# First attention of a 256-token transformer: pairs of heads one by one, or in units of two pairs

## The chip, the cores and the metric

The kernel runs on one core of one Trainium2 chip. The metric is the device time of one execution in microseconds. Three runs of the kernel before took 984.9, 985.58 and 985.37 us, median 985.37.

## The reference, cut to what matters

Three blocks follow one another on a sequence of 256 tokens of width 1024: attention with an MLP, a recurrent block with an MLP, and a block with three mixers. The change touches only the first attention, with 16 heads of 64:

```python
qkv = jnp.einsum('bsd,de->bse', h, w_qkv).reshape(B, S, 3, N_HEADS, HEAD_DIM)
...
s = jnp.einsum('bqhd,bkhd->bhqk', q_c, k_band).astype(jnp.float32) * scale + bias
s = jnp.where(key_pos[None, None, None, :] >= 0, s, NEG_INF)
p = jax.nn.softmax(s, axis=-1).astype(v_band.dtype)
return jnp.einsum('bhqk,bkhd->bqhd', p, v_band)
...
return jnp.einsum('bsd,de->bse', o, w_o)
```

Its output is added to `h`. The normalised `mem_2`, needed much later, is split beside the attention.

## The kernel before

Weights arrive as tiles of 1 MB through five buffers. ScalarE rounds each half of a tile to `hi` (L837) and VectorE makes the rest `lo` (L1357); a product is hi times hi, hi times lo and lo times hi. A tile of `wk` or `wq` gives two blocks of 128 features, one a "half" (`half`, L340 and L348: eight matmuls of 512 columns, eight of 256); its result leaves the bank as a copy on ScalarE (`bt`, L868) and a sum on VectorE (`joined`, L1371 and L1373), then a scaling on GpSimd (L2004). A tile of `wo` is applied in two halves of twelve matmuls of 512 columns (L295 to L297) that add into banks 0 to 3.

Five instruction streams are written by hand, one for each engine, and each engine runs its own strictly in its order; they meet at semaphores. A PSUM bank is claimed by `fill`, which makes TensorE wait until the reader of the bank's last content has released it.

The attention runs in nine steps over `ATTN_TILES` (three pairs of `wk`, `wq` tiles, then three `wo` tiles), two halves a step. Step j does, on TensorE (loop at L540): a half; the values of pair j - 2 (`pair_av`, L531, bank 7, 256 columns); the scores of pair j (`pair_scores`, L520, one head in bank 4, the other in bank 6); the three transposes of head 2j - 2 (`turn`, L470, bank 5); the other half; the transposes of head 2j - 1. A head's scores cover the causal part: 256 queries' worth in 384 columns. They pass through VectorE (bias and row minimum, L1490), ScalarE (exponential with sum, L922), VectorE (reciprocal and scaling, L1427 and L1430), TensorE (transposes), ScalarE (copy to `PT`, L927), TensorE (values), ScalarE (`oh`, L978) and VectorE (`ol`, L1476). Two buffers `L` and two `PT` hold one head each.

In every half the ScalarE stream (loop at L970) is: split a chunk of the coming weights, `bt` of this half, `oh`, the copy of transposes, the exponentials of one head, in steps 4 to 7 one square of `mem` (L879), which GpSimd adds up (L1999). The VectorE stream (loop at L1478) is: the `lo` chunk, bias and minimum of one head, `joined`, `ol`, in every second half `split_low` of `mem` (L1377), softmax of that head. After the ninth step come the values of pair 7, the sum of the squares of `mem` and the last `wo` tile.

Of the kernel before, what the change touches and what calls it, by code (L numbers as in the profile page):

```python
# [8 lines left out]
P = 128  # L9
S = 256  # L10
# [56 lines left out]
CROSS = [(256, 0), (0, 128), (384, 256), (128, 384)]  # L67
ROWS_ADDED = {"wo": 0, "w2_0": 4, "rout": 8, "w2_1": 12}
ATTN_TILES = [(name, i) for i in range(1, 4) for name in ("wk", "wq")] + [("wo", i) for i in range(3)]
DSA_STEPS = [[("dq", 3, 0), ("dq", 3, 1)], [("xq", 0, 0), ("xq", 0, 1)]]  # L70
DSA_STEPS += [[("xq", i, j)] for i in range(1, 4) for j in range(2)] + [[("gz", 0, 0)], [("gz", 0, 1)]]
INDEX_STEPS = [("dk", 0), ("dk", 1), ("dq", 0), ("dq", 1)]
# [18 lines left out]
def build(nc, A, out):  # L91
    ctx = ExitStack()

    def sem(name):
        return ctx.enter_context(nc.semaphore(name))
# [17 lines left out]
    h_added, ssq_made, ms_made, tok_rstd, hn_made = sem("h_added"), sem("ssq_made"), sem("ms_made"), sem("tok_rstd"), sem("hn_made")  # L113
    u_scaled, h_normed, bt_made = sem("u_scaled"), sem("h_normed"), sem("bt_made")
    sp_log, sp_made = sem("sp_log"), sem("sp_made")
    exp_made, p_made, o_high = sem("exp_made"), sem("p_made"), sem("o_high")
    z_made, z_high, z_low = sem("z_made"), sem("z_high"), sem("z_low")
    tap_made, xc_made, t_made = sem("tap_made"), sem("xc_made"), sem("t_made")
    gi_made, a_made, aa_made, mass_made, root_made, drive_made = (
# [23 lines left out]
    def place(name, off, free, dt=F32):  # L143
        return nc.alloc_sbuf_tensor_at(name, [P] + list(free), dt, offset=off)
# [8 lines left out]
    def slot(name, i, free=(NC, S), dt=F32, off=0):  # L153
        return place(name, o_slot[i] + off, free, dt)
# [46 lines left out]
    T = slot("T", 8, [16, 256])  # L201
    gw = slot("gw", 14, [2, NC, P])
    both = [place(f"both{i}", o_tmp + 2048 + 1536 * i, [384]) for i in range(2)]
    mk, mv = slot("mk", 3), slot("mv", 4, [2, D])
    bo = slot("bo", 6, [D], off=4096)
    zf = [slot(f"zf{i}", 5, [S], off=1024 * i) for i in range(4)]
# [66 lines left out]
    def pe():  # L273
# [192 lines left out]
        def turn(n, blocks, b=5):  # L466
            p.wait_ge(p_made, n + 1)
            done = fill(("turn", n), b)
            for src, dst in blocks:
                m = PE.transpose(bank[b][:, dst:dst + P], L[n % 2][:, src:src + P], ident[:, :])  # L470
            m.then_inc(done, 1)

        def weigh(n, o, V, a, b):
# [34 lines left out]
        cols("wq", 0, X2, (7, 6))  # L508
        for b in range(4):
            p.wait_ge(*free["wv", b])  # L510
        def pair_scores(j):

            p.wait_ge(kq_scaled, 4 * (j // 2) + 2 + j % 2)
            if j == 0:
                p.wait_ge(q_scaled, 1)
            done = [fill(("s", 2 * j + e), (4, 6)[e]) for e in range(2)]
            for a, b, n, c in ((P, S, S, 0), (0, P, P, 256)):
                for e in range(2):
                    r = slice(64 * e, 64 * e + 64)
                    m = PE.matmul(bank[(4, 6)[e]][:, c:c + n], q[r, j, a:b], k[r, j, 0:n], start=True, stop=True, skip_group_check=True)  # L520
                    if c:
                        m.then_inc(done[e], 1)

        def pair_av(j):
            for e in range(2):
                p.wait_ge(*free["turn", 2 * j + e])
            done = fill(("av", j), 7)
            for kb, c, e_ in ((0, 0, 256), (1, 256, 384)):
                for e in range(2):
                    n = 2 * j + e  # L530
                    m = PE.matmul(bank[7][64 * e:64 * e + 64, S - (e_ - c):S], v[:, kb, n * 64:n * 64 + 64], PT[e][:, c:e_],  # L531
                                  start=kb == 0, stop=kb == 1, skip_group_check=True)
            m.then_inc(done, 1)

        def wo(i, cs=(0, 1)):
            for k_ in range(2):
                p.wait_ge(freed[7], free["av", 2 * i + k_][1])
                rows("wo", i, 4, oh[:, 2 * i:2 * i + 2, :], ol[:, 2 * i:2 * i + 2, :], cs, (k_,), 0 if len(cs) == 1 else 1)

        for j in range(9):  # L540
            name, i = ATTN_TILES[j]
            if name == "wo":
                wo(i, (1,))
            else:
                half(name, i, 0, X2, 0)
            if j >= 2:
                pair_av(j - 2)
            if j < 8:
                pair_scores(j)
            if j:  # L550
                turn(2 * j - 2, CAUSAL)
            if j == 8:
                turn(15, CAUSAL, 4)
            if name == "wo":
                wo(i, (0,))
            else:
                half(name, i, 1, X2, 1)
            if 0 < j < 8:
                turn(2 * j - 1, CAUSAL)
        pair_av(7)  # L560
        total("mem", 7)
        wo(3)

# [253 lines left out]
    def act():  # L817
# [25 lines left out]
        def at_half(name, i, j):  # L843
            hi_to(2 * (T_OF[name, i] + HIS - 1) + j + 1)
# [80 lines left out]
        def turned(n, width):  # L925
            a.wait_ge(*full["turn", n])
            ACTE.activation(PT[n % 2][:, 0:width], bank_of["turn", n][:, 0:width], ACT.Copy).then_inc(free["turn", n][0], 1)  # L927
# [34 lines left out]
        for j in range(2):  # L962
            second("wq", j, scale=0.125)

        def turned_pair(n):
            if n >= 2:
                a.wait_ge(*full["av", n // 2 - 1])
            turned(n, 384)

        for j in range(9):  # L970
            name, t = ATTN_TILES[j]
            for e in range(2):
                at_half(name, t, e)
                if name != "wo":
                    second(name, 2 * t + e, scale=0.125 if name == "wq" else 1.0)
                if e == 0 and j >= 2:
                    a.wait_ge(*full["av", j - 2])
                    ACTE.activation(oh[:, j - 2, :], bank[7][:, 0:S], ACT.Copy).then_inc(o_high, 1)  # L978
                if e == 0 and j:
                    turned_pair(2 * j - 2)  # L980
                if e and j:
                    turned_pair(2 * j - 1)
                if j < 8:
                    n = 2 * j + e
                    a.wait_ge(*free["s", n])
                    soft(n, TT)
                if 4 <= j < 8:
                    square("mem", [mem[:, n, :] for n in range(NC)], 2 * (j - 4) + e)
        a.wait_ge(*full["av", 7])
        ACTE.activation(oh[:, 7, :], bank[7][:, 0:S], ACT.Copy).then_inc(o_high, 1)  # L990
        at_tile("wo", 3)
        inverse_root("mem")

# [184 lines left out]
        for i in range(10):  # L1178
            for name, t, j in DSA_STEPS[i]:
                at_half(name, t, j)  # L1180
                if name != "gz":
                    second(name, 2 * t + j, scale={"dq": 128 ** -0.5, "xq": 1.0 / 16}[name])
            if 1 <= i <= 8:
                n = i - 1
                a.wait_ge(*full[("av", 7) if n < 2 else ("dav", n - 2)])
                turned(16 + n, 384)
            if i < 8:
                a.wait_ge(*free["s", 16 + i])
                soft(16 + i, TT)
            n = i - 2  # L1190
            if n >= 0:
                a.wait_ge(*free["dav", n])
                ACTE.activation(yh[:, n, :], tmp[n % 2][:, :], ACT.Copy).then_inc(d_high, 1)
# [146 lines left out]
    def dve():  # L1340
# [23 lines left out]
        def at_half(name, i, j):  # L1364
            lo_to(2 * (T_OF[name, i] + 1) + j + 1)
# [105 lines left out]
        DVE.tensor_tensor(q[:, 0, :], q[:, 0, :], rstd["mix0"][:, :], ALU.mult).then_inc(q_scaled, 1)  # L1471
        joined(q[:, 1, :], "wq", 1, scale=0.125)

        def o_low(j):
            d.wait_ge(o_high, j + 1)
            DVE.tensor_tensor(ol[:, j, :], bank[7][:, 0:S], oh[:, j, :].bitcast(F32), ALU.subtract).then_inc(freed[7], 1)  # L1476

        for j in range(9):  # L1478
            name, t = ATTN_TILES[j]
            for e in range(2):  # L1480
                at_half(name, t, e)
                if j < 8:
                    i = 2 * j + e
                    Lb, s_ = L[e], stat[:, i % 16, :]
                    d.wait_ge(*full["s", i])
                    d.wait_ge(toep_cut, i // 4 + 1)
                    if j:
                        d.wait_ge(*full["turn", i - 2])
                    for m, (c, f, b0) in enumerate([(0, 256, 0), (256, 384, 128)]):
                        x = DVE.tensor_tensor_reduce(out=Lb[:, c:f], in0=bank_of["s", i][:, c:f], in1=T[:, i, b0:256], scale=-1.0,  # L1490
                                                     scalar=3.4e38, op0=ALU.add, op1=ALU.min, accum_out=s_[:, m:m + 1])
                    x.then_inc(free["s", i][0], 1)
                if name == "wk":
                    joined(k[:, 2 * t + e, :], "wk", 2 * t + e)
                if name == "wq":
                    joined(q[:, 2 * t + e, :], "wq", 2 * t + e, scale=0.125)
                if e == 0 and j >= 2:
                    o_low(j - 2)
                if e == 1 and j < 8:
                    split_low("mem", mem[:, j, :], mh, ml, "g_mem_2", j)  # L1500
                if j < 8:
                    soft(i, TT)
        o_low(7)
        lo_to(2 * (T_OF["wo", 3] + 2))
        by_token("mem", 2)

# [674 lines left out]
```

## Time and profile before

| | |
|---|---|
| median of 3 runs | 985.37 us |
| span of the profiled execution | 984.4 us |
| TensorE matmul busy in it | 977.1 us, 99% |
| VectorE, ScalarE, GpSimd busy | 682.6, 585.1, 66.2 us |
| mean granted TensorE clock | 0.998 |
| the attention's steps on TensorE | 42.6 to 111 us |

An engine's busy time is the sum of its instructions. The rows that follow further down come from five views: the page's chain (which work, followed back from the last instruction, made up the span), the same chain in order of time, stretches with the busy time of each engine, timelines of one engine, and groups of instructions by line. A matmul's row lasts longer than its step, since matmuls are pipelined, so in timelines the distance between starts is the cost.

### The profile page before, as it was taken

Reading aid. Unit: us, or ns where it says so; the run is one execution under the profiler, and the core shown is the slowest. Engines: PE = TensorE matmul, PEld = TensorE weight load, DVE = VectorE, ACT = ScalarE, POOL = GpSimd, SP = SyncE. Lnnn points to the kernel's source line nnn. Section 1 sums busy time; section 2 is a strip of 40 time slices with the busy share of each in tenths; the row PEclk is TensorE's granted clock in tenths of the full one; section 3 lists DMA queues with packets and bytes.
Section 4 is the critical chain, followed back from the end, with each engine's and each line's share of the span. In section 5 each row is a group of like instructions: output and inputs, shape, how many; then the busy total and the mean of one; then the engine's idle time right before and its main releaser. Section 6 shows DMA issues by size and latency. Waiting matters only on the chain.

```text
span 984.4 us, 13450 instructions
## 1 busy us (share of the span) xinstructions
PE 977.1 (99%) x5186; PEld 828.7 (84%) x5186; DVE 682.6 (69%) x1159; ACT 585.1 (59%) x1026; POOL 66.2 (7%) x80
## 2 busy tenths in 40 slices
PE   9999999999999999999999999999999999999997
PEld 6887888888888998888888888888888777988886
DVE  5887776655667889766556678778577355787564
ACT  6777755444547896654445476557766354685443
POOL 1323110000000241000000000000020000000000
PEclk9999999999999999999999999999999999999999
DMA  9753555554555445555645556445533543336551
GB/s 364 308 195 129 171 174 211 198 205 175 200 185 173 170 161 181 177 208 174 227 177 200 185 196 248 171 171 190 195 129 137 186 148 128 129 129 208 179 190 43
DMA packets 27119, 180.33 MB, mean 183 GB/s; under 512 B 2992, under 2 KB 3888, under 8 KB 6320
## 3 DMA queue, kind: packets, MB, share of 16 engines
q1 hardware_dynamic: 26336, 176.98, 50.3%
q0 software_dynamic: 288, 2.10, 0.6%
q8 instruction: 41, 0.67, 0.3%
q10 hardware_dynamic: 432, 0.39, 0.1%
q14 instruction: 22, 0.18, 0.0%
HBM read 178.41 MB, written 1.05 MB: 182 GB/s over the span
## 4 chain that ended last, share of the span: by engine, by line
PE 99%; DMA 1%; DVE 0%; ACT 0%; SPq 0%; issue 0%; DVEq 0%
PE bank L340 25%; PE bank L295 16%; PE bank L297 16%; PE bank L296 16%; PE bank L348 13%; PE bank L310 1%; PE bank L470 1%; PE bank L486 1%; PE bank L591 1%; PE bank L520 1%; PE bank L311 1%; PE bank L531 1%; DMA front<-in_front 1%; PE bank L462 1%; PE bank L706 0%; PE bank L722 0%
## 5 line engine op out<-in xcount | busy, mean ns | idle before, releaser
L1357 DVE TENSOR_TENSOR lo<-raw,hi 128x1024 fp32r<-128x1024 f32 x318 | 375.9, 1228 | 20.0 <-ACT hi L837 20.0
L837 ACT ACTIVATE hi<-raw 128x1024 fp32r<-128x1024 f32 x318 | 320.2, 1050 | 96.9 <-PE bank L297 95.1
L340 PE MATMUL bank<-X,hi 128*128 128x512 f32 x1016 | 267.0, 395 | 0.0
L340 PEld LDWEIGHTS bank<-X,hi 128*128 128x128 f32 x1016 | 185.0, 189 | 33.2 <-issue 0.4
L348 PEld LDWEIGHTS bank<-X,lo 128*128 128x128 f32 x1016 | 138.5, 190 | 10.1
L348 PE MATMUL bank<-X,lo 128*128 128x256 f32 x1016 | 141.6, 282 | 0.0
L868 ACT ACTIVATE bt<-bank 128x256 f32<-128x256 f32 x135 | 51.0, 380 | 142.7 <-PE bank L340 134.3
L1371 DVE TENSOR_TENSOR zr<-bank,bt 128x256 f32<-128x256 f32 x64 | 27.1, 424 | 109.0 <-ACT bt L868 109.0
L295 PE MATMUL bank<-hi,zh 128*128 128x512 f32 x256 | 100.0, 391 | 0.0
L297 PE MATMUL bank<-hi,zl 128*128 128x512 f32 x256 | 99.8, 390 | 0.0
L296 PE MATMUL bank<-lo,zh 128*128 128x512 f32 x256 | 99.6, 389 | 0.0
L295 PE MATMUL bank<-hi,X 128*128 128x512 f32 (+1 forms) x176 | 67.9, 386 | 0.0
L297 PE MATMUL bank<-hi,X 128*128 128x512 f32 (+1 forms) x176 | 66.9, 380 | 0.0
L296 PE MATMUL bank<-lo,X 128*128 128x512 f32 (+1 forms) x176 | 66.9, 380 | 0.0
L297 PEld LDWEIGHTS bank<-hi,zl 128*128 128x128 f32 x256 | 48.1, 188 | 10.4
L296 PEld LDWEIGHTS bank<-lo,zh 128*128 128x128 f32 x256 | 48.1, 188 | 10.2
L295 PEld LDWEIGHTS bank<-hi,zh 128*128 128x128 f32 x256 | 48.2, 188 | 8.9
L1012 ACT ACTIVATE zh<-zf 128x256 fp32r<-128x256 f32 x64 | 26.6, 415 | 21.2 <-DVE zf L1528 21.2
L297 PEld LDWEIGHTS bank<-hi,X 128*128 128x128 f32 x176 | 33.1, 188 | 6.4
L295 PEld LDWEIGHTS bank<-hi,X 128*128 128x128 f32 x176 | 33.1, 188 | 6.2 <-issue 0.3
L296 PEld LDWEIGHTS bank<-lo,X 128*128 128x128 f32 x176 | 33.1, 188 | 5.9
L922 ACT ACTIVATE L<-L,stat 128x256 f32<-128x256 f32 (+1 forms) x56 | 25.5, 456 | 20.4 <-DVE stat L1490 9.8
(344 smaller groups left out, 1428.3 us busy)
## 6 DMA issues: line engine op xcount, KB each, us to landing
raw<-in_w SPq DMA_DIRECT2D x64, 1024.0 KB, 4.7
raw<-in_rin SPq DMA_DIRECT2D x8, 1024.0 KB, 4.7
raw<-in_wk SPq DMA_DIRECT2D x4, 1024.0 KB, 11.0
raw<-in_wq SPq DMA_DIRECT2D x4, 1024.0 KB, 9.4
raw<-in_wo SPq DMA_DIRECT2D x4, 1024.0 KB, 4.7
raw<-in_mk SPq DMA_DIRECT2D x4, 1024.0 KB, 4.8
raw<-in_mv SPq DMA_DIRECT2D x4, 1024.0 KB, 4.7
raw<-in_rout SPq DMA_DIRECT2D x4, 1024.0 KB, 4.8
```

The lines of the kernel that those rows point to most:

```text
L295: PE.matmul(o, ah, bh, start=start, stop=False)
L296: PE.matmul(o, ah, bl, start=False, stop=False)
L297: return PE.matmul(o, al, bh, start=False, stop=stop)
L310: PE.matmul(bank[b][:, :], wh[:, c:c + P], both_, start=k_ == 0, stop=False, skip_group_check=True)
L340: return PE.matmul(bank[b][:, :], wh[:, c:c + P], x[:, k_, :, :].rearrange("p a b -> p (a b)"), start=k_ == 0, stop=k_ == NC - 1, skip_gro ...
L348: PE.matmul(bank[b][:, 0:S], wl[:, c:c + P], x[:, k_, 0, :], start=False, stop=False, skip_group_check=True)
L837: ACTE.activation(hi[u_ % HIS][:, c], raw[u_ % RAW][:, c], ACT.Copy).then_inc(hi_cut, 1)
L868: ACTE.activation(bt[n % BT][:, :], bank_of[key][:, S:2 * S], func, scale=scale, **kw).then_inc(bt_made, 1)
L922: i = ACTE.activation(Lb[:, c:e], Lb[:, c:e], ACT.Exp, scale=-1.0, bias=s_[:, m:m + 1], accum_out=s_[:, 2 + m:3 + m])
L1012: ACTE.activation(zh[i % 3][:, j, :], zf[c % 4][:, :], ACT.Copy).then_inc(z_high, 1)
L1357: DVE.tensor_tensor(lo[u_ % RAW][:, c], raw[u_ % RAW][:, c], hi[u_ % HIS][:, c].bitcast(F32), ALU.subtract).then_inc(lo_cut, 1)
L1371: DVE.tensor_tensor(dst, first, rest, ALU.add).then_inc(free[key][0], 1)
```

## The change

The 18 halves are numbered x. Heads now go in units: pairs (0, 1), (2, 3), (4, 5), (6), (7). A unit's scores are issued together, the first pair's in banks 4 and 6, the second's in banks 2 and 3, at x = 1, 5, 9, 13 and, for the last, 14. The values of a unit are issued together at x = 5, 9, 13, 16 and 17, 512 columns of bank 7 for two pairs; ScalarE's `oh` and VectorE's `ol` take them in one instruction each, with a semaphore `o_low` for `wo` and bank 7. There are four buffers for probabilities and four for their transposes (`L4`, `PT4`), the new ones where `hx` was. Transposes stand at the ends of halves or, for the last head of a unit, in the middle of one; the tables say where. VectorE and ScalarE take heads by the table `HEADS_AT`. The mixer that follows waits for unit 4 instead of pair 7. The core of the diff:

```diff
+ATTN_UNITS = [(0, 1), (2, 3), (4, 5), (6,), (7,)]
+UNIT_OF = {j: u for u, pairs in enumerate(ATTN_UNITS) for j in pairs}
+SCORES_AT = {1: (0, 1), 5: (2, 3), 9: (4, 5), 13: (6,), 14: (7,)}
+HEADS_AT = {1: (0,), 2: (1, 2), 3: (3,), 5: (4,), 6: (5, 6), 7: (7,), 9: (8,), 10: (9, 10), 11: (11,), 13: (12,), 14: (13,), 15: (14, 15)}
+TURN_IN = {5: 3, 9: 7, 13: 11, 16: 13, 17: 15}
+TURN_AT = {3: ((0, 5),), 4: ((1, 5), (2, 4)), 7: ((4, 5),), 8: ((5, 5), (6, 4)), 11: ((8, 5),), 12: ((9, 5), (10, 4)),
+           15: ((12, 5),), 16: ((14, 4),)}
+UNIT_AT = {5: 0, 9: 1, 13: 2, 16: 3, 17: 4}
...
+    L4 = L + [slot(f"L{i}", 3, [512], off=2048 * (i - 2)) for i in (2, 3)]
+    PT4 = PT + [slot(f"PT{i}", 3, [512], off=2048 * i) for i in (2, 3)]
...
+            src_ = L4[n % 4] if n < 16 else L[n % 2]
             for src, dst in blocks:
-                m = PE.transpose(bank[b][:, dst:dst + P], L[n % 2][:, src:src + P], ident[:, :])
+                m = PE.transpose(bank[b][:, dst:dst + P], src_[:, src:src + P], ident[:, :])
...
-        def pair_scores(j):
+        def pair_scores(j, banks):
...
-            done = [fill(("s", 2 * j + e), (4, 6)[e]) for e in range(2)]
+            done = [fill(("s", 2 * j + e), banks[e]) for e in range(2)]
...
-        def pair_av(j):
-            for e in range(2):
-                p.wait_ge(*free["turn", 2 * j + e])
-            done = fill(("av", j), 7)
-            for kb, c, e_ in ((0, 0, 256), (1, 256, 384)):
-                for e in range(2):
-                    n = 2 * j + e
-                    m = PE.matmul(bank[7][64 * e:64 * e + 64, S - (e_ - c):S], v[:, kb, n * 64:n * 64 + 64], PT[e][:, c:e_],
-                                  start=kb == 0, stop=kb == 1, skip_group_check=True)
+        def unit_av(u):
+            pairs = ATTN_UNITS[u]
+            for n in range(2 * pairs[0], 2 * pairs[-1] + 2):
+                p.wait_ge(*free["turn", n])
+            done = fill(("av", u), 7, (o_low, u + 1))
+            for o, j in enumerate(pairs):
+                for kb, c, e_ in ((0, 0, 256), (1, 256, 384)):
+                    for e in range(2):
+                        n = 2 * j + e
+                        m = PE.matmul(bank[7][64 * e:64 * e + 64, o * S + S - (e_ - c):o * S + S], v[:, kb, n * 64:n * 64 + 64],
+                                      PT4[n % 4][:, c:e_], start=kb == 0, stop=kb == 1, skip_group_check=True)
             m.then_inc(done, 1)
...
+            for k_ in ks:
+                p.wait_ge(o_low, UNIT_OF[2 * i + k_] + 1)
...
-        for j in range(9):
-            name, i = ATTN_TILES[j]
-            if name == "wo":
-                wo(i, (1,))
-            else:
-                half(name, i, 0, X2, 0)
-            if j >= 2:
-                pair_av(j - 2)
-            if j < 8:
-                pair_scores(j)
-            if j:
-                turn(2 * j - 2, CAUSAL)
-            if j == 8:
-                turn(15, CAUSAL, 4)
-            if name == "wo":
-                wo(i, (0,))
-            else:
-                half(name, i, 1, X2, 1)
-            if 0 < j < 8:
-                turn(2 * j - 1, CAUSAL)
-        pair_av(7)
+        for x in range(18):
+            name, i = ATTN_TILES[x // 2]
+            e = x % 2
+            for part in range(2):
+                if part and x in TURN_IN:
+                    turn(TURN_IN[x], CAUSAL)
+                if name == "wo":
+                    wo(i, (1 - e,), (part,))
+                elif x in TURN_IN:
+                    half(name, i, e, X2, e, range(4 * part, 4 * part + 4))
+                elif part:
+                    half(name, i, e, X2, e)
+            for n, b in TURN_AT.get(x, ()):
+                turn(n, CAUSAL, b)
+            if x in UNIT_AT:
+                unit_av(UNIT_AT[x])
+            for o, j in enumerate(SCORES_AT.get(x, ())):
+                pair_scores(j, ((4, 6), (2, 3))[o])
...
+        def turned_head(n):
+            if n >= 4:
+                a.wait_ge(*full["av", UNIT_OF[n // 2 - 2]])
+            a.wait_ge(*full["turn", n])
+            ACTE.activation(PT4[n % 4][:, 0:384], bank_of["turn", n][:, 0:384], ACT.Copy).then_inc(free["turn", n][0], 1)
+
+        def head_soft(n):
+            Lb, s_ = L4[n % 4], stat[:, n, :]
+            a.wait_ge(*free["s", n])
+            for m, (c, e) in enumerate(TT):
+                i = ACTE.activation(Lb[:, c:e], Lb[:, c:e], ACT.Exp, scale=-1.0, bias=s_[:, m:m + 1], accum_out=s_[:, 2 + m:3 + m])
+            i.then_inc(exp_made, 1)
+
+        for x in range(18):
+            name, t = ATTN_TILES[x // 2]
+            e = x % 2
+            at_half(name, t, e)
+            if name != "wo":
+                second(name, 2 * t + e, scale=0.125 if name == "wq" else 1.0)
+            if x in TURN_IN:
+                turned_head(TURN_IN[x])
+            for n, _ in TURN_AT.get(x, ()):
+                turned_head(n)
+            if x in UNIT_AT:
+                pairs = ATTN_UNITS[UNIT_AT[x]]
+                a.wait_ge(*full["av", UNIT_AT[x]])
+                ACTE.activation(oh[:, pairs[0]:pairs[-1] + 1, :].rearrange("p a b -> p (a b)"), bank[7][:, 0:S * len(pairs)],
+                                ACT.Copy).then_inc(o_high, 1)
+            for n in HEADS_AT.get(x, ()):
+                head_soft(n)
+            if 8 <= x < 16:
+                square("mem", [mem[:, n, :] for n in range(NC)], x - 8)
...
+        def unit_low(u):
+            pairs = ATTN_UNITS[u]
+            r = slice(pairs[0], pairs[-1] + 1)
+            d.wait_ge(o_high, u + 1)
+            DVE.tensor_tensor(ol[:, r, :].rearrange("p a b -> p (a b)"), bank[7][:, 0:S * len(pairs)],
+                              oh[:, r, :].rearrange("p a b -> p (a b)").bitcast(F32), ALU.subtract).then_inc(o_low, 1)
+
+        def head_soft(n):
+            Lb, s_ = L4[n % 4], stat[:, n, :]
+            d.wait_ge(exp_made, n + 1)
+            step(DVE.reciprocal(s_[:, 4:6], s_[:, 2:4]))
+            own()
+            for m, (c, e) in enumerate(TT):
+                i = DVE.tensor_scalar(Lb[:, c:e], Lb[:, c:e], s_[:, 4 + m:5 + m], None, ALU.mult)
+            i.then_inc(p_made, 1)
+
+        for x in range(18):
+            name, t = ATTN_TILES[x // 2]
+            e = x % 2
+            at_half(name, t, e)
+            for i in HEADS_AT.get(x, ()):
+                Lb, s_ = L4[i % 4], stat[:, i, :]
+                d.wait_ge(*full["s", i])
+                d.wait_ge(toep_cut, i // 4 + 1)
+                if i >= 4:
+                    d.wait_ge(*full["turn", i - 4])
+                for m, (c, f, b0) in enumerate([(0, 256, 0), (256, 384, 128)]):
+                    y = DVE.tensor_tensor_reduce(out=Lb[:, c:f], in0=bank_of["s", i][:, c:f], in1=T[:, i, b0:256], scale=-1.0,
+                                                 scalar=3.4e38, op0=ALU.add, op1=ALU.min, accum_out=s_[:, m:m + 1])
+                y.then_inc(free["s", i][0], 1)
+            if name == "wk":
+                joined(k[:, 2 * t + e, :], "wk", 2 * t + e)
+            if name == "wq":
+                joined(q[:, 2 * t + e, :], "wq", 2 * t + e, scale=0.125)
+            if x in UNIT_AT:
+                unit_low(UNIT_AT[x])
+            if e == 1 and x < 16:
+                split_low("mem", mem[:, x // 2, :], mh, ml, "g_mem_2", x // 2)
+            for i in HEADS_AT.get(x, ()):
+                head_soft(i)
```

## Rows read from the trace of the kernel before

**Rows 1.** The page: chain that ended last, shares by engine.

```profile
PE 99%; DMA 1%; DVE 0%; ACT 0%; SPq 0%; issue 0%; DVEq 0%
```

**Rows 2.** Stretches: us; busy of PE, PEld, DVE, ACT, POOL; clock, DMA, GB/s.

```profile
42.60:111.00 68.40, 68.40 (x428) 54.74 (x428) 53.12 (x157) 48.49 (x126) 17.53 (x24) 1.00 0.47 165
```

**Rows 3.** The chain in order of time, in the stage: start, us, what.

```profile
43.54 1.82 PE bank L340 x7
...
56.62 0.80 PE bank L531 x8
57.42 0.85 PE bank L520 x8
58.28 0.48 PE bank L470 x3
58.76 1.62 PE bank L340 x7
...
61.56 0.33 PE bank L470 x3
```

**Rows 4.** Timeline of PE, a value group, then scores: start, us, what.

```profile
56.55 0.44 PE L531 MATMUL bank<-PT,v 128*64 128x256 f32 x2
56.82 0.39 PE L531 MATMUL bank<-PT,v 128*64 128x256 f32 x2
57.03 0.39 PE L531 MATMUL bank<-PT,v 128*64 128x128 f32 x4
57.35 0.49 PE L520 MATMUL bank<-k,q 64*128 64x256 f32 x2
```

**Rows 5.** The chain again: two groups of transposes behind values.

```profile
105.96 0.86 PE bank L470 x6
```

**Rows 6.** Timeline of PEld: the weight loads of that value group.

```profile
56.55 0.63 PEld L531 LDWEIGHTS bank<-PT,v 128*64 128x64 f32 x8 [0.26 <-issue]
```

**Rows 7.** Timeline of ACT: exponential, weight chunk, bt, copy of transposes.

```profile
51.50 0.51 ACT L922 ACTIVATE L<-L,stat 128x256 f32<-128x256 f32 x1 [0.30 <-DVE stat L1490]
...
52.39 1.04 ACT L837 ACTIVATE hi<-raw 128x1024 fp32r<-128x1024 f32 x1
53.51 0.38 ACT L868 ACTIVATE bt<-bank 128x256 f32<-128x256 f32 x1
53.84 0.49 ACT L927 ACTIVATE PT<-bank 128x384 f32<-128x384 f32 x1
```

**Rows 8.** Timeline of DVE: softmax, weight chunk, reduction, join, split.

```profile
52.52 0.17 DVE L1427 RECIPROCAL stat<-stat 128x2 f32<-128x2 f32 x1 [0.72 <-ACT L L922]
...
53.19 1.22 DVE L1357 TENSOR_TENSOR lo<-raw,hi 128x1024 fp32r<-128x1024 f32 x1
54.32 0.42 DVE L1490 CUSTOM_DVE_ANT_0 L<-bank,T 128x256 f32<-128x256 f32 x1
...
54.87 0.42 DVE L1373 SCALAR_TENSOR_TENSOR q<-bank,bt 128x256 f32<-128x256 f32 x1
55.21 0.48 DVE L1377 SCALAR_TENSOR_TENSOR M<-mem,vec,M 128x256 fp32r<-128x256 f32 x1
```

**Rows 9.** 512 columns: timeline of ACT; groups of DVE by line.

```profile
116.97 0.63 ACT L896 ACTIVATE junk<-h 128x512 f32<-128x512 f32 x1 [2.15 <-DVE h L1403]
...
L1403 DVE TENSOR_TENSOR h<-bank,h 128x512 f32<-128x512 f32 x4 | 2.5, 680 | 0.0
```

**Rows 10.** Timelines of POOL and DVE: a sum beside the softmax.

```profile
93.30 0.80 POOL L1999 TENSOR_TENSOR sq<-sq,sq 128x256 f32<-128x256 f32 x1 [1.36 <-ACT sq L879]
...
93.15 1.03 DVE L1430 TENSOR_SCALAR L<-L,stat 128x256 f32<-128x256 f32 x2
```

**Rows 11.** Stretches behind the last matmul; timeline of PE at the start.

```profile
978.00:981.00 3.00, 1.33 (x6) 0.75 (x5) 0.93 (x4) 1.18 (x4) 0.00 (x0) 1.00 0.16 59
981.00:984.40 3.40, 0.00 (x0) 0.00 (x0) 1.30 (x2) 0.00 (x0) 0.00 (x0) 0.55 0.41 154
...
1.33 3.78 PE L498 MATMUL bank<-warm 128*128 128x512 f32 x4 [1.33 <-POOL warm L2006]
```

More of the change, by code:

```diff
@@ L115, in build @@
     sp_log, sp_made = sem("sp_log"), sem("sp_made")
-    exp_made, p_made, o_high = sem("exp_made"), sem("p_made"), sem("o_high")
+    exp_made, p_made, o_high, o_low = sem("exp_made"), sem("p_made"), sem("o_high"), sem("o_low")
     z_made, z_high, z_low = sem("z_made"), sem("z_high"), sem("z_low")
@@ L519, in pair_scores @@
                     r = slice(64 * e, 64 * e + 64)
-                    m = PE.matmul(bank[(4, 6)[e]][:, c:c + n], q[r, j, a:b], k[r, j, 0:n], start=True, stop=True, skip_group_check=True)
+                    m = PE.matmul(bank[banks[e]][:, c:c + n], q[r, j, a:b], k[r, j, 0:n], start=True, stop=True, skip_group_check=True)
                     if c:
                         m.then_inc(done[e], 1)
-        def pair_av(j):
-            for e in range(2):
-                p.wait_ge(*free["turn", 2 * j + e])
-            done = fill(("av", j), 7)
-            for kb, c, e_ in ((0, 0, 256), (1, 256, 384)):
-                for e in range(2):
-                    n = 2 * j + e
-                    m = PE.matmul(bank[7][64 * e:64 * e + 64, S - (e_ - c):S], v[:, kb, n * 64:n * 64 + 64], PT[e][:, c:e_],
-                                  start=kb == 0, stop=kb == 1, skip_group_check=True)
+        def unit_av(u):
[9 more added lines that the diff above has]
+                                      PT4[n % 4][:, c:e_], start=kb == 0, stop=kb == 1, skip_group_check=True)
@@ L533, in pair_av, with wo @@
             m.then_inc(done, 1)
-        def wo(i, cs=(0, 1)):
-            for k_ in range(2):
-                p.wait_ge(freed[7], free["av", 2 * i + k_][1])
+        def wo(i, cs=(0, 1), ks=(0, 1)):
+            for k_ in ks:
+                p.wait_ge(o_low, UNIT_OF[2 * i + k_] + 1)
                 rows("wo", i, 4, oh[:, 2 * i:2 * i + 2, :], ol[:, 2 * i:2 * i + 2, :], cs, (k_,), 0 if len(cs) == 1 else 1)
-        for j in range(9):
-            name, i = ATTN_TILES[j]
-            if name == "wo":
-                wo(i, (1,))
-            else:
-                half(name, i, 0, X2, 0)
-            if j >= 2:
-                pair_av(j - 2)
-            if j < 8:
-                pair_scores(j)
-            if j:
-                turn(2 * j - 2, CAUSAL)
-            if j == 8:
-                turn(15, CAUSAL, 4)
-            if name == "wo":
-                wo(i, (0,))
-            else:
-                half(name, i, 1, X2, 1)
-            if 0 < j < 8:
-                turn(2 * j - 1, CAUSAL)
@@ L963, in act @@
             second("wq", j, scale=0.125)
[L965 to L988, printed above, removed]
@@ L989, in act @@
-        a.wait_ge(*full["av", 7])
-        ACTE.activation(oh[:, 7, :], bank[7][:, 0:S], ACT.Copy).then_inc(o_high, 1)
+        def turned_head(n):
[9 more added lines that the diff above has]
+            i.then_inc(exp_made, 1)
@@ L1184, in act @@
                 n = i - 1
-                a.wait_ge(*full[("av", 7) if n < 2 else ("dav", n - 2)])
+                a.wait_ge(*full[("av", 4) if n < 2 else ("dav", n - 2)])
                 turned(16 + n, 384)
@@ L1472, in dve @@
         joined(q[:, 1, :], "wq", 1, scale=0.125)
[L1474 to L1502, printed above, removed]
@@ L1503, in dve @@
-        o_low(7)
+        def unit_low(u):
[12 more added lines that the diff above has]
+            i.then_inc(p_made, 1)
```

## The prediction

> **What bounds the kernel now.** I read the chain that ended last first: TensorE holds 99% of it [rows 1]. Then the table of stretches: from 42.6 to 111 us, the stage that the change rewrites, TensorE is busy in all of the 68.40 us at granted clock 1.00, with VectorE at 53 us and ScalarE at 48 [rows 2]. The view of waits names no matmul of this stage that waits for another engine. So the stage lasts as long as the sum of TensorE's steps, and every wait that is put into TensorE's stream is added to the run, because nothing behind it has slack. The question is what the change takes off these steps and where it makes TensorE wait for an engine that was hidden until now.
>
> The chain in order of time shows the rhythm of one pair [rows 3]: values (AV) 0.80, scores (S) 0.85, transposes (T) 0.48, a half of a weight tile 2.80 (58.76 to 61.56), T again, 0.33, another half. A pair takes 8.09 us.
>
> **What regrouping takes off TensorE.** The count of matmuls stays. What changes is how often TensorE goes from full tiles to half tiles and back. Inside a value group the starts lie 0.27, then 0.21 apart, and the two short passes with the exit take 0.32 [rows 4]. A pass over 256 columns in its stride is thus 0.21 and one over 128 half of that, 0.11: a pair run on behind another of its kind should take 0.64. An AV group then carries 0.80 - 0.64 = 0.16 of switching, an S group 0.85 - 0.64 = 0.21, and T behind S 0.48 - 0.33 = 0.15. Where S is followed by a half instead, the half's first seven matmuls take 1.82 instead of 1.62, so 0.20. Before there are 8 AV and 8 S groups, 7 of the S followed by T and 1 by a half. After it there are 5 of each (units of two, two, two, one, one), all S followed by halves.
> AV saves 3 x 0.16 = 0.48, S 3 x 0.21 = 0.63, and the exits 7 x 0.15 + 0.20 - 5 x 0.20 = 0.25. Two more places have two T back to back, the second of which costs 0.38 instead of 0.33 (0.86 - 0.48) [rows 5]: minus 0.10. Sum: 1.26, call it 1.25 us. Bounds: 0.75 if run-on AV pairs keep their 0.16, 1.6 if exits cost no more than now.
>
> The Trainium skill speaks against a part of this: TensorE: Matmul & The Clock Gate (Part 3, The mechanism) says that a weight load overlaps a running matmul only where the row group differs. The value matmuls use all 128 rows, so by that rule their loads would lie bare and a second AV pair would still cost 0.80, which makes the saving 0.75. Against it stands the trace, where eight such loads are busy 0.63 us under one AV group whose passes still start 0.21 apart [rows 6]; I go by the trace.
>
> **What the new order makes TensorE wait for.** I number the halves x = 0 to 17. Two things move: the T of a unit's last head now stands in the middle of the half right ahead of the unit's AV, and four heads' scores come at once into four banks while VectorE and ScalarE take them one or two per half.
>
> (1) x = 5 and x = 9. TensorE: four k of the half, T(3) (or 7), four k, then the AV of both pairs, which needs the copy PT of that last head. ScalarE's own order at that x is: split the next weight chunk, then `bt` of this same half, and only then the copy of T. `bt` needs the half's last matmul. So the copy can't start before the half has ended, though T ended 1.4 us earlier. Results appear 0.17 after the next matmul could have started (a matmul's 0.40 against a step of 0.23), then `bt` 0.33 (53.51 to 53.84), the copy 0.49 [rows 7], and about 0.1 for the two signals: 1.1 us, of which 0.1 is the entry step that was counted. 1.0 us each, 2.0 together. Before, a whole half of 2.80 and more lay between this T and its AV. Behind the waiting AV stand the scores and the next half; ScalarE and VectorE have nothing else to do in the meantime. This one I hold for nearly sure: bounds 0.8 and 1.3 each.
>
> (2) x = 12. The scores of pair 5 lie in banks 2 and 3, and `wo` opens banks 2 and 3 at x = 12. Head 11 leaves bank 3 by VectorE's reduction, which stands in VectorE's block 11. Count from the end of the scores at x = 9. TensorE: two halves, T(8), and three matmuls into bank 2: 2.80 + 2.80 + 0.33 + 3 x 0.23 (seven matmuls of 512 columns take 1.62) [rows 3] = 6.6. VectorE, from -0.5 (the first pair's scores are done early): reduction 0.55, join 0.34, difference of 512 columns 0.68, split 0.48, softmax 0.67 [rows 8, 9], which makes 2.2. The square of `mem` runs on GpSimd beside it, and where it does the two multiplications of the softmax take 1.03 instead of 0.55 [rows 10]: 2.7. Then the weight chunk 1.13, heads 9 and 10 reduced 1.10, which ends at 4.9. ScalarE starts head 9's exponentials at 4.4 and takes 0.90 a head [rows 7], so head 10's end at 6.2; its softmax 0.67 to 1.15, the next chunk 1.13, head 11's reduction 0.55: 8.5 to 9.0. Wait 1.9 to 2.4. Before, each half had one head; now three heads' work stands between these scores and bank 3. I take 2.0 (bounds 0.5 and 2.5, since small overlaps make it shorter).
>
> (3) x = 14. Pair 7 takes the same banks 4 and 6 as pair 6 one half earlier. TensorE has 12 matmuls of `wo` between, 2.8, and the entry, 0.1. VectorE has: reduction 12 at 0.1, 0.55; the difference 0.68; split 0.48; softmax 0.67 to 1.15; weight chunk 1.13; reduction 13, 0.55: 4.2 to 4.6 [rows 8 to 10]. Wait 1.3 to 1.7; I take 1.5 (bounds 0.5 and 1.8).
>
> (4) x = 16. From the end of T(12) ScalarE does its copy 0.49, two heads' exponentials 1.8, a square (256 columns, as `bt`) 0.4, a weight chunk 1.0 and the copy of T(13) 0.49, with signals 4.3. TensorE does 6 matmuls, T(13), 6 matmuls, T(14): 1.4 + 0.33 + 1.4 + 0.33, and wants the values of pair 6 at 3.5. Wait 0.7 to 0.8, I take 0.7 (bounds 0 and 1.2). At x = 13 the same sum comes out without a wait, since the wait at x = 12 has let ScalarE catch up; x = 17 has only one copy ahead of it.
>
> What is late next: after each wait VectorE and ScalarE have caught up, as the four sums above include; the weight chunks stay a tile ahead on ScalarE and half a tile on VectorE, and the loads of weights wait for TensorE's use of tiles, which comes in the same order. The new semaphore `o_low` costs nothing: `wo` reads a unit only half a unit later. One copy and one difference of 512 columns instead of two of 256 [rows 9] saves these engines about 0.1 each per unit, which is off TensorE's path.
>
> **Sum.** 1.0 + 1.0 + 2.0 + 1.5 + 0.7 = 6.2 us of waits against 1.25 saved: +4.95. The profiled span is 984.4, so 989.35; the runs' median, 985.37, stands 1.0 above that span, so **990.3 us**, 0.5% slower.
>
> **Rivals.**
> A, the forecast, 988.3 to 991.8: all five waits come as counted, give or take the bounds. Chance 0.63.
> B: the banks come free in time and only the two copies behind `bt` wait: +2.0 - 1.25 = +0.75, 986.1. For it: VectorE is busy 53 of 68 us only, and every chain of (2) to (4) starts from an adding up of many steps. Against: these idle times lie where an engine waits for the other, and the chain of one softmax through both engines does not get shorter. 0.15.
> C, the other side: not slower. The deeper buffers hide all copies, as four instead of two buffers suggest, and only the switching is seen: 984.1. It decides at the point where ScalarE's copy of T(3) comes ahead of the half's end; the code's order speaks against it. With exits as cheap as now 983.8, and only something unseen in the steps could take it under 983.4. 0.10.
> D: the clock falls at the wait of x = 12. After the last matmul, which ended 1.33 us behind 978, the stretch from 981 shows a mean clock of 0.55: it fell in a pause of some two microseconds or more. At the start four passes of 512 columns take 3.78 us, about double of what 0.21 per 256 makes (1.7) [rows 11]. If it fell once and stayed down for some 4 us of work, as long as these four passes, that costs 1.9 more: 992.2. Against: the longest wait that I count is 2.0, at the near edge of that pause. 0.12.
>
> **Chances and range.** A difference of 0.2%, 983.4 to 987.3, is about what a measurement of this kernel can tell. Faster: 0.04 out of C. Same: 0.06 of C and 0.12 of B. Slower: A, D and the rest of B, 0.78. The range has to take in A, B and most of D: 985.9 to 992.6, with C and the far end of D left out.
>
> **What would show it.** In the profile of after, TensorE's rows at the first AV group should carry an idle time of about 1 us, released by ScalarE's PT copy, twice; `wo`'s fourth matmul an idle time released by VectorE's reduction; the scores of pair 7 the same; and AV runs of 16 passes should take 1.44 and S runs 1.49 in the chain. No idle at the AV would put me wrong on (1) and make it C; idle at the AV alone makes it B; a column PEclk under 1.00 in the stage makes it D. A saving other than 1.25 shows in the lengths of the groups themselves.

## The result, and the profile after

| | before | after |
|---|---|---|
| runs, median (lowest to highest) | 985.38 us (984.9 to 985.58, 4 runs) | 991.26 us (990.35 to 992.22, 4 runs) |
| ratio to before, 95% interval | | 1.0059 (1.0047 to 1.0072) |
| span of the profiled execution | 984.4 us | 989.0 us |
| the stage on TensorE (below) | 67.69 us | 72.44 us |

The change makes the kernel slower by 0.6%, where 0.5% was forecast (990.3 us).

The stage is measured in the chain, from the first scores to the sum of the squares of `mem`. Before it is

```profile
42.69 0.85 PE bank L520 x8
...
110.38 0.63 PE bank L458 x2
```

67.69 us from start to start. After it is

```profile
45.41 1.51 PE bank L531 x16
...
115.05 0.63 PE bank L468 x2
```

69.64, and the half of a tile that now stands ahead of the first scores, 2.80, belongs to it: 72.44, or 4.75 more. From there to the last matmul both kernels take 868.6 us. The whole loss lies in the stage.

The kernel before was not quite free of waits here. Its view of waits names no matmul, but two weight loads of L295 with 0.3 us each. One timeline row of such a load, and the two steps of the chain that are longer than the usual 0.23:

```profile
95.37 0.19 PEld L295 LDWEIGHTS bank<-hi,oh 128*128 128x128 f32 x1 [0.28 <-DVE lo L1357]
...
95.52 0.35 PE bank L295
103.65 0.36 PE bank L295
```

The timeline puts the first down to the `lo` chunk of VectorE and ties the second to no event; a `lo` chunk (102.18, 1.21 long) ends just ahead of that one too. Together they cost 0.25 us, which is needed below.

The view of waits of the kernel after has these (engine, line, what released it: us in total, times, longest):

```profile
PE bank L531 <- DVE stat L1517: 1.9, 1, 1.9
PE bank L544 <- issue: 1.8, 2, 0.9
PE bank L305 <- DVE stat L1517: 1.4, 1, 1.4
...
PE bank L544 <- ACT PT L979: 0.5, 1, 0.5
```

The scores of pair 7 wait for VectorE's reduction (x = 14), two value groups wait 0.9 each (x = 5 and 9), `wo`'s fourth matmul waits for a reduction (x = 12), the values of pair 6 for a copy (x = 16). The timelines of TensorE at x = 5 and x = 12 (start, us, what, idle before and releaser):

```profile
59.25 0.39 PE L350 MATMUL bank<-X,hi 128*128 128x512 f32 x1
60.54 1.52 PE L544 MATMUL bank<-PT,v 128*64 128x256 f32 x16 [0.90 <-issue]
...
86.85 0.40 PE L307 MATMUL bank<-hi,ol 128*128 128x512 f32 x1
88.67 0.51 PE L305 MATMUL bank<-hi,oh 128*128 128x512 f32 x1 [1.42 <-DVE stat L1517]
```

The cost of a wait is the distance of the starts less the ordinary step. At x = 5 that is 1.29 - 0.33 = 0.96; "issue" there means that the profile ties the wait to no event, but ScalarE's timeline shows what TensorE stood for:

```profile
59.68 0.38 ACT L878 ACTIVATE bt<-bank 128x256 f32<-128x256 f32 x1 [0.91 <-PE bank L350]
59.96 0.48 ACT L979 ACTIVATE PT<-bank 128x384 f32<-128x384 f32 x1
```

ScalarE is idle for 0.91 until the half ends, does `bt`, then the copy, which ends at 60.44; TensorE goes on at 60.54. At x = 12 the cost is 1.82 - 0.23 = 1.59, and the next step is 0.11 longer than usual in restarting.

What answers to [rows 3] in the chain after: the value and score groups of two pairs, and two groups of transposes in a row.

```profile
55.85 0.66 PE bank L481 x6
...
60.54 1.52 PE bank L544 x16
62.06 1.51 PE bank L531 x16
```

### The profile page after: what moved, and what is told of

Same layout as the page of the kernel before. It is cut to its first block, busy times and chain, and to the rows that moved or that the text cites. A ratio compares the mean times of both kernels' runs of the same rounds, so it can differ in the third digit from the quotient of the medians.

```text
span 989.0 us, 13441 instructions
## 1 busy us (share of the span) xinstructions
PE 976.4 (99%) x5186; PEld 829.2 (84%) x5186; DVE 683.1 (69%) x1156; ACT 583.7 (59%) x1023; POOL 69.3 (7%) x80
## 3 DMA queue, kind: packets, MB, share of 16 engines
HBM read 178.41 MB, written 1.05 MB: 181 GB/s over the span
## 4 chain that ended last, share of the span: by engine, by line
PE 97%; DVE 1%; ACT 1%; DMA 1%; issue 0%; SPq 0%; DVEq 0%
PE bank L350 25%; PE bank L305 16%; PE bank L307 16%; PE bank L306 16%; PE bank L358 13%; PE bank L320 1%; PE bank L481 1%; PE bank L497 1%; PE bank L601 1%; PE bank L321 1%; PE bank L544 1%; DMA front<-in_front 1%; PE bank L472 1%; PE bank L531 1%; PE bank L716 0%
## 5 line engine op out<-in xcount | busy, mean ns | idle before, releaser
L1561 DVE TENSOR_TENSOR zl<-zf,zh 128x256 fp32r<-128x256 f32 x64 | 26.9, 421 | 4.8 <-ACT zh L1028 3.3
```

What stands on the lines that cost most here:

```text
L1561: DVE.tensor_tensor(zl[i % 3][:, j, :], zf[c % 4][:, :], zh[i % 3][:, j, :].bitcast(F32), ALU.subtract).then_inc(z_low, 1)
```

## The experiments

Each starts from the kernel after the change unless it says otherwise. "Stage" is measured as above, 72.44 in the kernel after. All edits stand at the same places of the three loops.

**The copy ahead of `bt`.** ScalarE:

```diff
             at_half(name, t, e)
+            if x in (5, 9):
+                turned_head(TURN_IN[x])
             if name != "wo":
                 second(name, 2 * t + e, scale=0.125 if name == "wq" else 1.0)
-            if x in TURN_IN:
+            if x in TURN_IN and x > 9:
                 turned_head(TURN_IN[x])
```

> The kernel after the change, with one edit in ScalarE's order: at x = 5 and x = 9 the copy of the transposes of heads 3 and 7 comes ahead of `bt` of the same half. Theory (TensorE waits there only because the copy stands behind `bt`): both idle times of 0.90 us ahead of the value groups vanish, a value group starts 0.33 us behind the half's last matmul, and the span falls from 989.0 by 2 x 0.96 to about 987.1. Rival (the copy is late for another reason, or the time is lost again further on, at the banks of x = 12 and 14): the span stays near 989.0, with longer waits at `wo` and at the scores of pair 7.

Measured: the wait at x = 5 is gone (a step of 0.33), that at x = 9 is down to 0.10; the stage falls by 1.83 to 70.61, and the waits of 1.4, 1.9 and 0.5 stay as they are. The span is 988.1, since the opening of this execution was longer: its first scores start at 46.30, not 45.41, behind a wait of 2.0 for the first weights. The runs give 989.18 (988.29 to 992.65). The order on ScalarE is the cause of these two waits, and in the stage nothing of them comes back.

**The other banks.** TensorE:

```diff
-                pair_scores(j, ((4, 6), (2, 3))[o])
+                pair_scores(j, ((2, 3), (4, 6))[o] if x == 9 else ((4, 6), (2, 3))[o])
```

> The kernel after the change, with one edit in TensorE's stream: at x = 9 the scores of pair 4 go to banks 2 and 3 and those of pair 5 to banks 4 and 6, so that heads 8 and 9, which VectorE takes first, lie in the banks that `wo` opens at x = 12. Theory (the wait of 1.42 us idle ahead of `wo`'s fourth matmul is bank 3, held by head 11): it vanishes, 1.69 us. But that wait has also let ScalarE catch up: added up from the trace of after, the copy of T(9) then ends 0.2 after T(11) wants bank 5, and the copy of T(11) 0.45 after the values of unit 2 could start, so 0.65 comes back at x = 13 and the span is 988.0. Rival (waits are independent): nothing comes back and the span is 987.3. Rival (VectorE's lag, not the bank, is what counts): no gain, 989.0.

Measured: `wo`'s fourth matmul waits no more, but the seventh does, for the low part of its weight chunk. It starts 0.58 behind the sixth in place of 0.23:

```profile
87.56 0.50 PE L305 MATMUL bank<-hi,oh 128*128 128x512 f32 x1 [0.19 <-DVE lo L1373]
```

With 0.11 for the longer step behind it that costs 0.46, so the bank was worth 1.24 of 1.70. Something did come back, but at x = 12 and from VectorE; the two waits that I had added up for x = 13 did not appear. The expectation's size was nearly right (1.05) and its mechanism wrong. The stage of this execution is 72.74 all the same: behind the wait at x = 14 its clock fell, which is told below. The runs give 990.27.

**Head 13 together with head 12.**

```diff
-HEADS_AT = {... 13: (12,), 14: (13,), 15: (14, 15)}
+HEADS_AT = {... 13: (12, 13), 15: (14, 15)}
```

> The kernel after the change, with one edit in the table of heads: VectorE and ScalarE take head 13 together with head 12, at x = 13 instead of x = 14. Theory (the scores of pair 7 wait 1.9 us for bank 6, whose reduction stands behind softmax 12 and a weight chunk): that wait vanishes and the span is 987.1; the wait of 0.55 at x = 16 stays. Rival (the scores of pair 7 wait for something else, such as bank 4 or the scaling of q): 989.0.

Measured: no wait at the scores of pair 7, the others as before. The stage is 70.51, 1.93 less. The runs give 988.99 (988.38 to 989.31), 2.9 above the kernel before on the same chip, where the kernel after lay 5.9 above it at first and 5.05 when it was measured once more. The edit moves only the reduction that frees bank 6, so bank 6 was what they waited for.

**All three, and ScalarE's copies ahead of its weight chunk in the halves of `wo`** (x = 12, 13, 16 and 17; by the edit at x = 15 too).

> The kernel after the change with the three edits of the other runs together, and with ScalarE's copies of transposes ahead of its weight chunk at x = 12, 13, 16 and 17. The order of TensorE's work is that of after but for the banks. Theory (the change costs 6.1 us in waits and saves about 1.5 in switching between full and half tiles): all five waits go and the span is 984.4 - 1.5 = 982.9, faster than the kernel before by about 0.15%. Rival (the switching saves nothing, the small gap between waits and loss in after is something else): 984.4. Rival (ScalarE and VectorE can't keep up with this order anyway): new waits of a microsecond or more somewhere in the stage, 985 or above.

Measured: 985.6 us (985.47 to 985.68) against 986.1 for the kernel before on the same chip, ratio 0.9995 (0.9985 to 1.0004); span 984.2, stage 67.42. Not 982.9, since 1.20 us of smaller waits are left: the weight chunk at x = 12 (0.46), 0.13 and 0.10 at x = 9, 0.22 and 0.29 at x = 16. With these taken out, 67.69 + 1.20 - 67.42 = 1.47 is saved.

**What is left, first attempt.** From there: transposes in the middle of a half to bank 7, head 10 taken with head 11 at x = 11, exponentials ahead of the copy at x = 15.

> The last kernel (all three edits and copies ahead of the weight chunk), in whose trace 1.2 us of waits are left: 0.46 at x = 12 for the low part of a weight chunk (VectorE), 0.13 and 0.10 at x = 9, 0.22 and 0.29 at x = 16 (ScalarE's copies, bank 5). Edits: the transposes in the middle of a half go to bank 7 instead of 5; VectorE and ScalarE take head 10 with head 11 at x = 11; at x = 15 ScalarE does the exponentials of heads 14 and 15 ahead of the copy of T(12). Theory (the regrouping itself is worth 1.45, and what is left are waits): the span falls from 984.2 by 1.2 to about 983.0, 0.15% under the kernel before. Rival (each edit moves a wait on instead of taking it away): 984.0 or above.

Measured: 986.29 us against 985.85, ratio 1.0003 (0.9994 to 1.0011), stage 67.62. The waits at x = 12 (weight chunk) and the one of 0.29 at x = 16 went, that at x = 9 grew to 0.35, and a larger one came ahead of the transposes of head 10, which TensorE wants before its later softmax is done:

```profile
89.42 0.55 PE L481 MATMUL bank<-ident,L 128*128 128x128 f32 x3 [0.82 <-DVE L L1512]
```

The rival had it: this edit moved a wait on.

**What is left, second attempt.** From the kernel with all three edits again. The exponentials at x = 15 stay ahead of the copy, only T(13) goes to bank 7, and VectorE makes its weight chunk ahead of the softmax of head 10:

```diff
@@ TensorE
+                    turn(TURN_IN[x], CAUSAL, 7 if x == 16 else 5)
...
@@ VectorE, heads 9 and 10 at x = 10 again
             for i in HEADS_AT.get(x, ()):
+                if i == 10:
+                    at_half("wq", 3, 1)
                 head_soft(i)
```

> The kernel of e4_all with three smaller edits: VectorE makes the weight chunk of x = 11 ahead of the softmax of head 10 (its lateness was the wait of 0.46 at x = 12), ScalarE does the exponentials of heads 14 and 15 ahead of the copy of T(12), and T(13) goes to bank 7 (0.22 and 0.29 at x = 16). Heads 9 and 10 are taken together again, as in e4_all, since taking head 10 later cost 0.82 idle ahead of its transposes in e5_best. Theory (the regrouping is worth 1.45 and e4_all still waits 1.2): the stage, from the first scores to the sum of `mem`, falls by about 0.9 against e4_all, span 983.3. Rival (waits move on): 984.0 or above. Either way the difference to the kernel before is about 0.1%, near what the runs can tell.

Measured: 984.84 us (983.4 to 987.06) against 986.06, ratio 0.9988 (0.998 to 0.9997): faster than the kernel before by about 0.1%, the only version here whose interval lies under 1, if narrowly. The stage is 66.42 and has 0.23 of waits left, both at x = 9; 67.69 + 0.23 - 66.42 = 1.50 saved. In its chain the values of unit 0 stand right behind the half, and their two pairs take 1.45.

**The longer wait.** Three additions on VectorE whose result nobody reads:

```diff
                 Lb, s_ = L4[i % 4], stat[:, i, :]
+                if x == 14:
+                    for r in range(3):
+                        step(DVE.tensor_tensor(warm[:, :], T[:, 12:14, :].rearrange(...), T[:, 14:16, :].rearrange(...), ALU.add))
+                        own()
```

> The kernel after the change, with three extra additions of 512 columns on VectorE ahead of the reduction of head 13 at x = 14, whose result nobody reads: about 2.0 us. It makes the one wait at x = 14 longer, from 1.9 to 3.9. Theory (the wait holds TensorE, and in a longer one the clock falls to 1.2 GHz more surely): the wait is 3.9, the scores of pair 7 and the first matmuls of `wo` behind it take nearly twice their steps, which cost 1.6 where it was seen, and the span is 989.0 + 2.0 + 1.6 = 992.6 in nearly every run. Rival (the fall has nothing to do with the wait): granted clock 1.00 behind it, span 991.0.

Measured: the view of waits has 4.0 in place of 1.9, and in the stretches (us; busy of PE, PEld, DVE, ACT, POOL; clock; DMA) the clock falls within the wait and stays low behind it:

```profile
100.30:104.70 4.40, 0.42 (x2) 0.00 (x0) 4.20 (x9) 0.49 (x2) 0.35 (x1) 0.85 0.00 2
104.70:110.00 5.30, 5.25 (x17) 4.17 (x18) 3.83 (x13) 2.18 (x6) 0.80 (x1) 0.50 0.00 0
```

The stage is 77.12, 4.68 more; 2.18 is the longer wait, so the clock costs 2.50, more than the 1.6 expected. The runs are 995.3 us (994.72 to 995.74), ratio 1.0092, the spans 993.4 to 994.4.

**The narrow sums.** The root mean square of `mem` is left out but for one column:

```diff
-                POOL.tensor_tensor(sq[3][:, :], sq[3][:, :], sq[j % 3][:, :], ALU.add)...
+                w = slice(0, 1 if n0 else S)
+                POOL.tensor_tensor(sq[3][:, w], sq[3][:, w], sq[j % 3][:, w], ALU.add)...
```

> The kernel after the change, in which GpSimd adds up one column of the squares of `mem` instead of 256: the root mean square of `mem` is thus left out but for one column, and GpSimd's seven sums beside the softmax get short. Theory (the term of 0.48 by which a GpSimd sum lengthens VectorE's second multiplication of the softmax belongs into the wait of x = 14, but not into that of x = 12, since GpSimd's sums start only behind x = 11): the wait at x = 14 falls from 1.92 to 1.4, that at x = 12 stays at 1.69, span 988.5. Rival (the multiplication is long for another reason): both waits stay, 989.0.

Measured: as expected. The wait at x = 14 is 1.4 idle in place of 1.9 and costs 1.44 in place of 1.92; at x = 12 it stays 1.4 idle. Span 988.5, stage 71.93; the runs give 989.92 (989.0 to 990.47). VectorE's two multiplications of head 12, which take 1.03 in the kernel after, here:

```profile
98.87 0.55 DVE L1503 TENSOR_SCALAR L<-L,stat 128x256 f32<-128x256 f32 x2
```

**The kernel after once more.**

> The kernel after the change, unchanged, for the spread of its runs beside the others. Theory (its clock falls in some executions at the wait of 1.9 us at x = 14): spans of 989 to 991, two or more groups about 1.6 apart. Rival (the spread comes from elsewhere): as narrow as that of the kernel with head 13 taken early, 987.1 to 988.0 there, 0.9 us wide.

Measured: 990.9 us (990.5 to 992.19), ratio 1.0054 (1.0041 to 1.0066). The spans are 990.7, 990.9, 989.6, 989.2 and 989.5: two groups about 1.4 apart, with mean clock 0.998 in the first two and 1.00 in the others. The profiled execution is one of the first group. Its timeline behind the wait at x = 14, and its stretch, against the same stretch of the kernel after in the execution of the first section:

```profile
102.00 0.92 PE L531 MATMUL bank<-k,q 64*128 64x256 f32 x8 [1.85 <-DVE stat L1517]
103.44 0.63 PE L306 MATMUL bank<-lo,oh 128*128 128x512 f32 x1
103.87 0.63 PE L307 MATMUL bank<-hi,ol 128*128 128x512 f32 x1
...
102.80:106.20 3.40, 3.40 (x11) 2.71 (x9) 3.26 (x11) 1.32 (x3) 0.80 (x1) 0.50 0.00 0
```

```profile
102.80:106.20 3.40, 3.40 (x18) 2.81 (x18) 3.37 (x13) 1.30 (x3) 0.80 (x1) 1.00 0.00 0
```

Eleven matmuls in place of 18 in the same 3.4 us, steps of 0.43 in place of 0.23. The waits are the same as in the other execution, and the stage is 73.99, so this costs 1.55. The bank experiment agrees: 72.44 less 1.24 for the bank, but 72.74 measured, 1.54 more.

## Why the prediction was right, point by point

| | forecast | measured |
|---|---|---|
| saved by regrouping | 1.25 (0.75 to 1.6) | 1.50, with 0.25 of waits in the kernel before |
| (1) x = 5, x = 9 | 1.0, 1.0 | 0.96, 0.97 |
| (2) x = 12 | 2.0 (0.5 to 2.5) | 1.70 |
| (3) x = 14 | 1.5 (0.5 to 1.8) | 1.92 |
| (4) x = 16 | 0.7 (0 to 1.2) | 0.56 |
| not forecast: transposes of head 7 | 0 | 0.14 |
| sum of the waits | 6.2 | 6.25 |
| span | 989.35 | 989.0 |
| median of the runs | 990.3 | 991.26 |

The saving is the stage before plus the waits less the stage after: 67.69 + 6.25 - 72.44 = 1.50. The same sum gives 1.51 with head 13 taken early, 1.47 and 1.50 in the two kernels with most waits taken out. But 0.25 of it are the two waits of the kernel before for a `lo` chunk, which are not switching. 1.25 is left for what the forecast counted, and the waits are its price.

**The saving.** So the sum of 1.25 was met, and the 1.50 differs from it by a term that the forecast lacked: the prediction read that no matmul of the stage waited, and missed the rows of the two weight loads. The timelines give the parts. Eight value groups of 0.80 became three of 1.45 and two of 0.80: 0.44, where 0.48 was forecast. Eight score groups of 0.85 to 0.86 became three of 1.51 and two of 0.85: 0.60, where 0.63 was forecast. 0.21 is left for the exits, where 0.25 less 0.10 was forecast. A run of two value groups takes 1.45, and two score groups 1.51, where 1.44 and 1.49 were worked out: the pair that runs on behind another costs its passes and nothing more. A second value pair costs 0.65 (1.45 - 0.80), against the Trainium skill's rule on weight loads (TensorE: Matmul & The Clock Gate, Part 3, The mechanism), by which it would have been 0.80; the trace decides. Two groups of transposes take 0.66, twice 0.33: the 0.05 which I had charged for the second one, at two places, belongs to a place behind values. And one exit I had not counted: the values of pair 6 are followed by a half now, whose first step is 0.43 in the chain instead of 0.23, so 0.20; before, transposes followed them, for 0.15. I had one term too dear by 0.10 and another too cheap by 0.05, and about 0.07 too much in the two groups, so that the sum came out is in part luck.

**(1)** was right in mechanism and size; the copy moved ahead of `bt` takes it away.

**(2)** had the right bank and the right engine. The term that was mis-sized is the slow multiplication: I added 0.48 for a sum on GpSimd at x = 9 and x = 10. But GpSimd does its scalings of q and k first, in its own order, and the first of these sums starts at 89.90, behind the wait. With 2.2 instead of 2.7 for the first part, the rest of my own sum ends at 8.0 instead of 8.5, and less TensorE's 6.6 that makes 1.4; the idle time is 1.42. By the distance of the starts it costs 1.59, and 0.11 for the longer step behind it, so 1.70. The narrow sums leave this wait as it is.

**(3)** had 4.2 to 4.6 for VectorE's chain, and here the sums do run beside it: 0.48 in full, as the narrow sums show. I took the middle. In the trace VectorE's chain takes 4.7 from the end of pair 6's scores (97.01 to 101.73), and 0.15 more pass until TensorE starts, which I had left out. The wait is 1.92, just over the bound of 1.8.

**(4)** was 0.14 too high, as instructions in a row on ScalarE follow more closely than their durations: the two exponentials and the copy ahead of them start 0.39, 0.88 and 0.88 apart.

**Rival D came true in part.** The clock falls, not at x = 12 but at the slightly longer wait of x = 14, and not in every execution. Where it falls it costs 1.55, against the 1.9 that I had from [rows 11]. That helps to explain why the span of the profiled execution, which was not touched by it, agrees within 0.4 and the median lies 1.0 above the forecast: forecast and rival were not alternatives, they add. The spans of the four executions are 989.0, 989.5, 990.4 and 990.9, their middle 0.6 above the forecast of 989.35. The other 0.35 is the step from span to run: I took 1.0, and in the four runs after the change it is 1.3. The four passes of the opening were a weak witness: the stretches give 1.00 for 1.3 to 5 us too, and only their length speaks for a low clock there. I should have weighed the fall for every wait of about two microseconds, and for a part of the runs.

**The sum of the waits** was closer than its terms: they were off by -0.07 for (1), -0.30, +0.42, -0.14 and, for the transposes of head 7, +0.14, which cancel to 0.05. The mechanism of each was right, the closeness of 6.2 to 6.25 was luck. The bounds of the five waits and of the saving add up to 986.4 to 992.7, so the 988.3 to 991.8 of forecast A was narrower than its own terms allow.

**Rival B** asked for banks that come free in time: the waits at x = 12 and 14 rule it out. **Rival C** is ruled out for this version, and the last experiments show what it takes to get there: the edits of four waits, for 0.1%.

## What to carry to other kernels

Where one engine is always busy, add up its steps for what a regrouping saves, and then write down for each place where it now needs another engine's result what that engine does in its own order before it: an engine that serves its stream strictly in turn can start on an input that came early only when the instructions ahead of it are done. Work that is issued in larger groups keeps each bank and buffer longer, so look for the next claim of every bank that a group fills. Five waits of 0.56 to 1.92 us cost four times what the grouping saved here; and a version with the waits taken out is the way to learn whether the grouping was worth anything. When a saving is read as a difference, look for small waits in the kernel before as well: the rows of weight loads showed two that the rows of matmuls did not.

## What the runs showed of the hardware

Behind a wait of TensorE of 1.85 us its granted clock fell from 2.4 to 1.2 GHz in some executions and not in others, at the same place of the same kernel: in the profiled execution of the bank experiment and of the repeated kernel it fell (0.50 for 3.4 us), in the profiled execution after the change it did not. The waits of 0.9 and 1.4 us left it at 1.00 in all profiles here, and so did one of 1.96 us in the opening of the first experiment. With head 13 taken early, where that wait is gone, it stayed at 1.00. With a wait of 4.0 it fell during the wait, and was low for 5.3 us of work behind it. The Trainium skill states (TensorE: Matmul & The Clock Gate, Part 1, What's actually happening) that the two states of the clock are 1.2 and 2.4 GHz; the stretches agree, with 0.50 and 1.00. The wait at x = 14 need not be the only place of a fall: of 50 executions of the kernel before, which has no such wait, three have spans of 986.7 to 987.2 with a mean clock of 0.997 or 0.998, against a median of 984.7 or 984.8 on the same chips. None of them was profiled, so where their time went is not shown.

A GpSimd sum of 256 columns beside VectorE's multiplications makes these take 1.03 instead of 0.55. VectorE's subtraction of 1024 columns is longer beside such sums too: where four of them follow one another, from 89.90, two subtractions take 3.42 us together, and 2.35 with the narrow sums. A subtraction that starts when the sum has ended takes 1.21.
